# A two-layer hybrid trunk on one core: the second mixer's front in another order of ScalarE and VectorE, and the first mixer's recurrence with fewer VectorE operations

## The reference, cut to what matters

```python
for layer in range(2):
    h = h + (even_mixer if layer == 0 else odd_mixer)(rmsnorm(h, mix_norm[layer]))
    h = h + squared_relu_mlp(rmsnorm(h, mlp_norm[layer]))
return rmsnorm(h, final_norm)

# even_mixer: p = h @ w_in; attention; conv + silu on q, k; then in chunks of 128 tokens
C_loc = einsum('bnlh,bnlhk,bnlhv->bnhkv', wgt, kc, vc)              # n_loc alike, without v
C, m = exp(gl + m - m_new) * C + exp(ml - m_new) * C_loc, m_new     # state before each chunk
w_intra, w_inter = exp(dlog - m_t), exp(b + m_prev - m_t)
qk = (qc @ kc^T) * w_intra
num = qk @ vc + w_inter * (qc @ C_prev)
den = sum(qk) + w_inter * (qc @ n_prev)
hm = num / max(|den|, exp(-m_t))                                    # per head
y_ml = head_layernorm(hm) * ml_norm * sigmoid(o)                    # mean and variance over 128
return concat(y_att, y_ml) @ w_out

# odd_mixer: z, xbc, dt, (r, k, v, wd, ad, gd) = parts of h @ w_in
xbc = silu(causal_conv(xbc)); y = ssd_chunked(xs, dt, A, B, C) + d * xs; y_ssm = norm(y * silu(z))
rw = rw + (token_shift(rw) - rw) * mu
decay = exp(-exp(w_log(tanh(wd) @ w2))); a = sigmoid(a0 + ad @ a2)
kk = kh * k_k / max(sqrt(sum((kh * k_k)**2)), 1e-12); kh = kh * (1 + (a - 1) * k_a)
S = S * w_t - (S @ kk_t) b_t + v_t k_t;  y_t = S @ r_t              # b = kk * a
y_rw = (head_layernorm(y) + bonus) * g
return concat(y_ssm, y_rw) @ w_out
```

## Time and profile before

| | |
|---|---|
| median of 3 runs | 1412.69 us (1411.59 to 1414.43) |
| the profiled execution | 1419.52 us, its span 1417.7 us |
| TensorE busy | 1335.1 us (94% of the span), 6461 matmuls |
| VectorE, ScalarE, GpSimd busy | 582.6, 530.9, 657.2 us |
| granted clock over the span, share of full speed | 0.966 |

### The profile page before, as it was taken

One profiled execution on the slowest core, in us unless ns is written; L12 is line 12 of the kernel. 1 busy time (PEld: TensorE's weight loads), 2 busy tenths in 40 slices (PEclk: granted clock), 3 DMA queues, 4 the chain that ended last, 5 costly groups with the idle time before them and its releaser, 6 DMA issues.

```text
span 1417.7 us, 17835 instructions
## 1 busy us (share of the span) xinstructions
PE 1335.1 (94%) x6461; PEld 1072.1 (76%) x6461; DVE 582.6 (41%) x957; ACT 530.9 (37%) x860; POOL 657.2 (46%) x810
## 2 busy tenths in 40 slices
PE   5999968999999999999788998888999999999998
PEld 4777656788888888887467877788878888888886
DVE  4537676421211212345588576364442121121233
ACT  5335643332322413436553534533343132232332
POOL 5653213664554555564335431321355555554552
PEclk9999978999999999999898998999899999999999
DMA  9322101333333333332212310000133333323321
GB/s 273 90 75 60 60 1 43 91 90 99 94 90 90 102 89 89 98 95 75 60 44 61 90 48 28 1 1 2 45 90 104 90 92 102 89 89 102 91 89 60
DMA packets 198034, 109.12 MB, mean 77 GB/s; under 512 B 4570, under 2 KB 195280, under 8 KB 197840
## 3 DMA queue, kind: packets, MB, share of 16 engines
q1 hardware_dynamic: 197552, 108.16, 26.2%
q0 software_dynamic: 416, 0.07, 0.0%
HBM read 106.11 MB, written 2.10 MB: 76 GB/s over the span
## 4 chain that ended last, share of the span: by engine, by line
PE 71%; DVE 9%; ACT 3%; issue 2%; POOL 0%; DVEq 0%; ACTq 0%; POOLq 0%
PE ps L862 20%; PE ps L863 20%; PE ps L864 20%; PE ps L849 1%; PE ps L903 1%; PE ps L904 1%; PE ps L905 1%; DVE late L2471 1%; DVE arena L2255 1%; PE ps L1278 1%; PE ps L1289 1%; PE ps L1267 1%; PE ps L1146 1%; PE ps L1264 1%; PE ps L1332 0%
## 5 line engine op out<-in xcount | busy, mean ns | idle before, releaser
L771 POOL TENSOR_TENSOR w_lo<-raw_w,w_hi 128x256 fp32r<-128x256 f32 x760 | 613.4, 839 | 620.4 <-ACT w_hi L1386 620.4
L1386 ACT ACTIVATE w_hi<-raw_w 128x1024 fp32r<-128x1024 f32 x190 | 201.1, 1058 | 553.2 <-PE ps L864 441.1
L862 PE MATMUL ps<-hn_hi,w_hi 128*128 128x512 f32 x880 | 359.2, 408 | 11.2 <-POOL w_lo L771 9.5
L863 PE MATMUL ps<-hn_lo,w_hi 128*128 128x512 f32 x880 | 351.7, 400 | 0.0
L864 PE MATMUL ps<-hn_hi,w_lo 128*128 128x512 f32 x880 | 351.3, 399 | 0.0
L862 PE MATMUL ps<-hid_hi,w_hi 128*128 128x512 f32 x576 | 228.4, 397 | 0.0
L863 PE MATMUL ps<-hid_lo,w_hi 128*128 128x512 f32 x576 | 228.3, 396 | 0.0
L864 PE MATMUL ps<-hid_hi,w_lo 128*128 128x512 f32 x576 | 228.3, 396 | 0.0
L862 PEld LDWEIGHTS ps<-hn_hi,w_hi 128*128 128x128 f32 x880 | 167.6, 190 | 61.5 <-issue 18.8
L863 PEld LDWEIGHTS ps<-hn_lo,w_hi 128*128 128x128 f32 x880 | 167.5, 190 | 41.8 <-issue 2.9
L864 PEld LDWEIGHTS ps<-hn_hi,w_lo 128*128 128x128 f32 x880 | 167.5, 190 | 40.9
(11 more groups left out here) (371 smaller groups left out, 1365.5 us busy)
## 6 DMA issues: line engine op xcount, KB each, us to landing
raw_w<-in_w_up SPq DMA_DIRECT2D x64, 512.0 KB, 4.0
raw_w<-in_w_down SPq DMA_DIRECT2D x64, 512.0 KB, 3.7
raw_w<-in_o_w_in SPq DMA_DIRECT2D x27, 512.0 KB, 3.7
raw_w<-in_e_w_in SPq DMA_DIRECT2D x19, 512.0 KB, 3.8
raw_w<-in_e_w_out SPq DMA_DIRECT2D x8, 512.0 KB, 3.7
raw_w<-in_o_w_out SPq DMA_DIRECT2D x8, 512.0 KB, 3.5
rwkv_raw<-in_x SPq DMA_DIRECT2D x4, 512.0 KB, 8.1
out<-arena SPq DMA_DIRECT2D x8, 256.0 KB, 2.9
```

What stands on the lines that cost most here:

```text
L771: nc.gpsimd.tensor_tensor(w_lo[:, n % CUT, ks], raw_w[:, n % RING, ks], w_hi[:, n % CUT, ks].bitcast(F32), ALU.subtract).then_inc(w_cut, 1)
L862: mm(o, a_hi, b_hi, start=(k == 0), stop=False)
L863: mm(o, a_hi, b_lo, start=False, stop=False)
L1386: A(w_hi[:, n % CUT], raw_w[:, n % RING], ACT.Copy).then_inc(w_high, 1)
```

## The change

**First mixer.** `inter` is added in PSUM onto `num`. For that q carries its weight beforehand: ScalarE takes the exponential straight from `m_row` (`q_exp`, four operations for each of chunks 1, 2, 3) and GpSimd multiplies it with q. The denominators and the moments are read in PSUM, and the division is taken into the gain that ScalarE applies when it writes the normalised chunk (`ml_normed`, four operations). `c_loc` takes one bank, its state one to three operations. `k_tok` is turned inside the attention's steps and `k_w` is made from PSUM by two operations. ScalarE's copies of the attention half stand ahead of the sigmoid, VectorE's `low_first` behind `ml_weights(0)`. Lower half tile 0 of the out projection stands behind chunk 1, and half tiles 1, 2 and 3 behind chunk 3, all ahead of the turns of `y_ml`.

**Second mixer.** The LoRA products, gates and decays come a slot or so earlier, the sum for kk's norm one slot earlier; VectorE takes slots 9 and 10 among the receptance parts, the first four channels' silu is one slot later on ScalarE, the last steps of the substitution and its two transposes stand ahead of `take_staged(17)`, and the multiplication by z's silu stands behind the first chunk's solve instead of ahead of it. The other banks move with the round-robin.

```diff
+        if u == 9:
+            for a in range(2):
+                yield "k_tok", a
+        if u == 7:
+            yield "q_exp", 1
...
-    behind = {0: [("norm", 2), ("norm_tok",)], 1: [("turn", ("dt",))], 3: [("lora", 0)],
-              4: [("lora", 1), ("lora", 2), ("a_cum",)], 5: [("lora", 3)], 7: [("kk_sum",)],
+    behind = {0: [("norm", 2), ("norm_tok",)], 1: [("turn", ("dt",))], 3: [("lora", 0), ("lora", 1)],
+              4: [("lora", 2), ("lora", 3), ("a_cum",)], 6: [("kk_sum",)],
...
+    out_banks = [[0, 7, 5, 6, 1, 2, 3, 4], list(range(8))]
+    turned_banks = [[1, 2, 3, 4], [4, 5, 6, 7]]
...
+                for par in range(2):
+                    put("num", n, par, bank=1 + 2 * (n % 2) + par)
+                if n == 1:
+                    put_out(0, 0)
+            for j in range(1, 4):
+                put_out(0, j)
+            put_turned(0, "y_ml")
...
+                        for t in range(1, NT):
+                            pool.wait_ge(S["wi_made"], t)
+                            nc.gpsimd.tensor_tensor(q_w[:, t - 1], q_w[:, t - 1], conv_out[:, 0:2, t * P:(t + 1) * P],
+                                                    ALU.mult).then_inc(S["q_weighted"], 1)
...
-                            ins = mm(o[:, par * 129:(par + 1) * 129], qkw[:, n % 2, hh * P:(hh + 1) * P],
-                                     v_ml[:, n, hh, :], start=True, stop=True)
+                            ins = mm(o[par][:, a * 129:(a + 1) * 129], qkw[:, n % 2, hh * P:(hh + 1) * P],
+                                     v_ml[:, n, hh, :], start=(a == 0), stop=(n == 0), skip_group_check=True)
...
+                        pe.wait_ge(S["q_weighted"], n)
...
-                                ins = mm(o[par][:, a * 129:(a + 1) * 129], conv_out[r, a, tok], c_state[r, n, a, :],
-                                         start=True, stop=True)
+                                ins = mm(o[par][:, a * 129:(a + 1) * 129], q_w[r, n - 1, a, :], c_state[r, n - 1, a, :],
+                                         start=False, stop=True, skip_group_check=True)
...
-                for j in range(3):
+                                    close(ins, "num", n, par)
+                    if n == 1:
+                        half_tile(0, 0, 0)
+                for j in range(1, 4):
                     half_tile(0, j, 0)
                 pe.wait_ge(S["y_ml_gated"], NT - 1)
                 pe.wait_ge(S["y_ml_ready"], 1)
                 for f in range(4):
                     turn(("y_ml", f), [o_gate[:, n, f * P:(f + 1) * P] for n in range(NT)])
-                half_tile(0, 3, 0)
...
+                elif kind == "q_exp":
+
+                    act.wait_ge(S["wl_ready"], u + 1)
+                    o = full(act, "m_row", u).rearrange("p (a b t) -> p a b t", a=2, b=2)
+                    for a in range(2):
+                        for par in range(2):
+                            r = slice(64 * par, 64 * par + 64)
+                            hh = 2 * a + par
+                            ins = A(q_w[r, u - 1, a, :], o[r, a, par, :], ACT.Exp, scale=-1.0,
+                                    bias=marr[r, u, hh:hh + 1])
+                    ins.then_inc(free_sem("m_row", u), 1)
+                    drained(act, "m_row", u)
+                    act.sem_inc(S["wi_made"], 1)
...
+            for u in range(8):
+                drained(act, "att", u)
+            for k in range(4):
+                A(hid_hi[:, k, :], y_mix[:, k, :], ACT.Copy).then_inc(high, 1)
...
+            def ml_normed(n):
+
+                act.wait_ge(S["ml_normed"], n + 1)
+                for par in range(2):
+                    o = full(act, "num", n, par)
+                    for a in range(2):
+                        j = 4 * n + 2 * par + a
+                        ins = A(w_ml[:, n, 2 * a + par, :], o[:, a * 129:a * 129 + P], ACT.Identity, scale=mv[:, j, 1:2],
+                                bias=mv[:, j, 0:1])
+                    ins.then_inc(free_sem("num", n, par), 1)
...
+                ml_root(n)
+                ml_normed(n)
...
                 if j == 3:
                     act.wait_ge(S["omka_ready"], 1)
                     gates_of(0)
+                    gates_of(1)
                 if j == 4:
-                    gates_of(1)
                     gates_of(2)
+                    gates_of(3)
                 if j == 5:
-                    gates_of(3)
                     decay_exps(0)
+                    decay_exps(1)
                 if j == 6:
-                    decay_exps(1)
                     decay_exps(2)
-                if j == 7:
                     decay_exps(3)
                     A(e_s, e_a, ACT.Exp, scale=-DECAY_K).then_inc(S["scales"], 1)
...
-                    drained(act, "bonus")
                     A(a_turned[0:64, :], o[0:64, 0:P], ACT.Copy).then_inc(free_sem("a_turn"), 1)
-                if j == 14:
+                if j == 15:
...
+                        link(V.tensor_tensor(c_tmp, c_state[:, n - 1], over(keep_gain[:, n, :], 2, 129), ALU.mult))
+                    o = full(dve, "c_loc", n)[:, 0:258].rearrange("p (a v) -> p a v", a=2)
+                    if n:
+                        for a in range(2):
+                            ins = V.scalar_tensor_tensor(out=c_state[:, n, a, :], in0=o[:, a, :],
+                                                         scalar=new_gain[:, n, a:a + 1], in1=c_tmp[:, a, :],
                                                          op0=ALU.mult, op1=ALU.add)
...
+            def ml_moments(n):
...
+                o = [full(dve, "num", n, par)[:, 0:258].rearrange("p (a v) -> p a v", a=2) for par in range(2)]
+                for par in range(2):
+                    ins = V.tensor_scalar(d2[:, par, :].unsqueeze(2), o[par][:, :, P:P + 1], -1.0, None, ALU.mult)
...
+                link(V.tensor_tensor(d2, d2, em_arg[:, n, :].rearrange("p (a b) -> p b a", b=2), ALU.max))
+                V.reciprocal(d, d)
+                for par in range(2):
+                    for a in range(2):
+                        ins = V.bn_stats(st6[:, 2 * par + a, :], o[par][:, a, 0:P])
+                link(ins)
+                for j in range(4):
+                    ins = V.bn_aggr(mv[:, 4 * n + j, :], st6[:, j, :])
+                link(ins)
+                var = mv[:, 4 * n:4 * n + 4, 1]
+                link(V.tensor_tensor(var, var, d, ALU.mult))
+                V.tensor_tensor(var, var, d, ALU.mult).then_inc(S["hm_done"], 1)
+
+            def ml_gains(n):
+
+                mean, gain = mv[:, 4 * n:4 * n + 4, 0], mv[:, 4 * n:4 * n + 4, 1]
+                dve.wait_ge(S["ln_root"], n + 1)
+                link(V.reciprocal(gain, gain))
+                link(V.tensor_tensor(gain, gain, dn[:, n % 2, :], ALU.mult))
+                V.scalar_tensor_tensor(out=mean, in0=mean, scalar=-1.0, in1=gain, op0=ALU.mult, op1=ALU.mult
+                                       ).then_inc(S["ml_normed"], 1)
             ml_weights(0)
+            for k in range(4):
+                low_first(0, k, y_mix[:, k, :])
             for n in range(NT):
                 if n + 1 < NT:
                     ml_weights(n + 1)
-                if n == 2:
-                    for k in range(4):
-                        low_first(0, k, y_mix[:, k, :])
-                ml_combine(n)
                 if n:
-                    ml_out(n - 1)
-            ml_out(NT - 1)
+                    ml_gains(n - 1)
+                ml_moments(n)
+            ml_gains(NT - 1)
+            drained(dve, "num", NT - 1, 0)
+            drained(dve, "num", NT - 1, 1)
+            dve.wait_ge(S["o_gained"], NT)
+            V.tensor_tensor(o_gate[:, NT - 1, :], o_gate[:, NT - 1, :], w_ml[:, NT - 1].rearrange("p h t -> p (h t)"),
+                            ALU.mult).then_inc(S["y_ml_ready"], 1)
...
             running_decay(0)
+            running_decay(1)
             take_staged(3)
             shift(3)
-            running_decay(1)
...
             key_part(3)
+            take_staged(9)
             receptance_part(0)
+            conv_staged(9)
             receptance_part(1)
-            take_staged(9)
+            take_staged(10)
             receptance_part(2)
-            receptance_part(3)
-            conv_staged(9)
...
-            take_staged(10)
+            receptance_part(3)
...
-            substitute(23, 24)
+            substitute(23, 31)
+            V.transpose(inv_rows, sub_inv.rearrange("p t c -> p c t"))
+            link(V.transpose(inv_cols, sub_inv))
+            dve.sem_inc(S["inv_ready"], 1)
...
-            substitute(28, 31)
-            V.transpose(inv_rows, sub_inv.rearrange("p t c -> p c t"))
-            link(V.transpose(inv_cols, sub_inv))
-            dve.sem_inc(S["inv_ready"], 1)
...
-            for n in range(NT):
-                drained(dve, "z_tok", n)
-                V.tensor_tensor(xs_tok[:, n, :], xs_tok[:, n, :], z_tok[:, n, :], ALU.mult).then_inc(S["z_silu"], 1)
-            dve.wait_ge(S["z_silu"], NT)
...
```

(5 more changed lines are left out.)

214 lines of the change are left out of this document (74 added, 140 removed).

## The result

The changed kernel has a median of 1399.28 us over 4 runs (1397.91 to 1401.18), beside 1413.56 for the kernel before: 14.3 us less, a ratio of 0.9895 (95% interval 0.9871 to 0.9920). The forecast was 1386, with 1375 to 1401 as its range. The sign and the places were right; the size was 26.6 us where 14.3 came, outside the forecast's own range of 1380 to 1393 and inside the wider one that takes the rivals in.

The account below looks back on a forecast made before the run. TensorE's matmuls, one behind the other, held 71% of the chain, so only other engines' places in it could be shortened. Gains 7.6 + 9.4 + 9.6 = 26.6 off 1412.7 gave 1386 us, range 1380 to 1393, with rivals 1375 to 1401.

Parts of the forecast that it names:

- A: First mixer: ScalarE and two numerators' ring cause TensorE waits of 5 us or more at num(2), num(3); 1392, chance 0.13.
- B: Second mixer's front: bound by VectorE's work, not its waits; only kk's part and the end gain; 1395, chance 0.14.
- D: Slower: in the tighter front, VectorE's 128x512 operations beside GpSimd cost 0.45 us more each; 1418 at 70, chance 0.04.
- First mixer, 7.6 predicted: First mixer: VectorE no longer last, upper half tiles start at 226.0 instead of 233.6; gain 7.6 us, bounds 2 and 12.
- the walk: First mixer: step-by-step timing of the new chain through ScalarE, VectorE and TensorE, from attention's tail to upper half tiles at 226.0.
- the rule on PSUM operands: First mixer's bn_stats: PSUM reads put at 0.07 us more each; at a doubling, 0.22 each, the gain would be 5.8.
- Second mixer up to slot 14, 9.4 predicted: Second mixer's front: fewer waits bring b_tok's turn from 794.25 to 784.8 us; gain 9.4, bounds 3 and 14.
- (a): Second mixer's front: kk_sum, last decays and root one slot earlier bring kk_inv to 696.2 from 698.69; 2.5 us.
- (b): Second mixer, from kk_inv: VectorE's waits for block copies and conv scaling go; 6.7 less 0.5 of new waits, 6.2 us.
- (c): Second mixer's front: a further 0.7 us of waits that follow also goes, bringing b_tok's turn to 784.8.
- The cover for the substitution: Second mixer: some 7 us of moved steps and transposes cost nothing, as VectorE idles 16.84 us before 818.93.
- Behind slot 26, 9.6 predicted: Second mixer's end: 5.85 us of waits, 2.9 of clock and about 0.9 in the first solve go; 9.6, bounds 6 and 11.

Follow-up runs that it names:

- first_reorder: Changed kernel with low_first behind ml_weights(1) and half tile 0 behind chunk 2's first products (qk_st, c_loc): 1394.35 us, ratio 0.9858 to the kernel before.
- kk_ahead: Changed kernel with VectorE's reciprocal of kk's norm ahead of shift(6) instead of behind it: 1395.90 us, ratio 0.9865 to the kernel before.
- silu_mid: Changed kernel with the first four channels' silu right behind ScalarE's cut at slot 15, ahead of the scaling: 1402.90 us, ratio 0.9919 to the kernel before.
- sub_less: Changed kernel with ten of the 31 substitution steps (10 to 19) left out, so part of the computation is missing: 1391.59 us in one run.
- no_end: Changed kernel with substitution steps and transposes spread as before and z's product ahead of the first solve again: 1410.98 us, ratio 0.9955 to the kernel before.
- no_front: Changed kernel with the second mixer's order of before from slot 3 to 15, its end as changed: 1404.04 us, ratio 0.9912 to the kernel before.
- sub_spread: Changed kernel with only the substitution's last steps and transposes spread over slots 17 to 21 again: 1404.21 us, ratio 0.9910 to the kernel before.
- z_ahead: Changed kernel with only z's product ahead of the first solve again: 1409.89 us, ratio 0.9955 to the kernel before.
- best2: Changed kernel with low_first behind ml_weights(1), half tile 0 behind chunk 2's first products, and kk's reciprocal ahead of shift(6): 1394.16 us, ratio 0.9850.
- pool_light: Changed kernel with GpSimd's first-mixer product of the gate with ml_norm cut to 8 of 512 columns: 1398.73 us in one run.

## Why the prediction came out as it did

The median of 1399.28 is 13 us above the forecast, and above the figures of rivals A (1392) and B (1395) too. A did not come: the waits at num(2) and num(3) were 3.87 and 3.24, under its 5. B came in part: behind kk_inv VectorE had hardly a wait for ScalarE left, and its work set the pace. D's sign did not come: VectorE's mean for 128x512 from kk_inv to b_tok's turn went from 0.82 to 0.83 us, not to 1.1. Term by term:

**First mixer, 7.6 predicted, 5.3 in the trace, 3.8 timed.** The mechanism was right: VectorE left the chain, the ring of two numerators made the new waits (3.87 and 3.24 where 3 each were said), the turns of y_ml came without a wait at full clock. Mis-sized were two steps of the walk. The attention's tail was put at 2 us later; TensorE finished it at 186.2 instead of 182.7, so 3.4. Part of this is the price of q_exp: four of its exponentials took 1.47 us and not the 1.2 that w_exp's price gave, 0.8 us more for the three.

```profile
173.57 1.47 ACT L1613 ACTIVATE rwkv_raw<-ps,small 64x128 f32<-64x128 f32 x4
```

And weights(1) stood behind the hid_hi copies and low_first until 193.7, which I had at 192. VectorE after, around it:

```profile
190.51 2.50 DVE L1899 TENSOR_TENSOR hid_lo<-y_mix,hid_hi 128x512 fp32r<-128x512 f32 x4 [2.03 <-ACT hid_hi L1626]
192.93 0.75 DVE L2167 SCALAR_TENSOR_TENSOR rwkv_raw<-ps,late 128x256 f32<-128x256 f32 x2
...
196.75 0.86 DVE L2203 BATCH_NORM_STATS2 small<-ps 128x6 f32<-128x128 f32 x4
...
198.06 1.05 DVE L2209 TENSOR_TENSOR small<-small 128x4 f32<-128x4 f32 x1
199.14 1.21 DVE L2210 TENSOR_TENSOR small<-small 128x4 f32<-128x4 f32 x1
200.85 0.75 DVE L2167 SCALAR_TENSOR_TENSOR rwkv_raw<-ps,late 128x256 f32<-128x256 f32 x2 [0.51 <-PE ps L1078]
```

inter(1) ended at 196.5, 3.5 late; the half tile behind it found the full clock from its fourth matmul and took 3.6 instead of 5, which gave 1.5 back. first_reorder turned both orders together, and 3.3 us came back; what each is worth alone, no run shows. The tiny products at 198 and 199 are slower than the 0.15 I gave them, but weights(2) then waited 0.51 for TensorE, so they cost nothing here. One reading was off: chunk 1's L2153 took 1.89 us in the kernel before, not the 1.18 of chunk 2, so the change took 0.7 more from VectorE than I counted.

The question put to the rule on PSUM operands is settled by L2203: four bn_stats from PSUM took 0.86, from SBUF 0.87. There was no price for these. The Trainium skill ("VectorE: DVE Perf Modes", "Rules for kernel authors") offers a copy to SBUF where many operations follow as the other choice beside the slower rate from PSUM; for these four reads the copy would have bought nothing.

**Second mixer up to slot 14, 9.4 predicted, 5.5 in the trace (10.8 less 5.3).** (a) kk's part was 1.3, not 2.5. The step that failed is "the sum still has to pass ScalarE [...] and the reciprocal": the walk let the reciprocal follow ScalarE's root at once, but it stood behind shift(6) in VectorE's queue, which waited 5.57 us for a scaling that ScalarE did only after the root and the next cut. VectorE after:

```profile
687.12 0.75 DVE L2264 SCALAR_TENSOR_TENSOR rwkv_raw<-relu,cols,rwkv_raw 128x512 f32<-128x512 f32 x1 [5.57 <-ACT rwkv_raw L1662]
...
688.77 3.34 DVE L2352 RECIPROCAL arena<-arena 8x512 f32<-8x512 f32 x1
```

The root had been done since 685.5, 9.3 us earlier than before. kk_ahead took 2.8 back. (b) From kk_inv to b_tok's turn 95.6 us became 91.3: 4.3, not 6.9. The waits that I named did go; VectorE's idle time over this stretch fell by 5.7, where I had 6.2. But its busy time rose by 1.5, from 78.04 to 79.49:

```profile
692.17:783.47 91.30, 84.83 (x385) 64.68 (x386) 79.49 (x116) 37.66 (x66) 40.13 (x41) 0.90 0.22 61
```

That is in part rival D's mechanism at a small scale: of its 68 operations of 128x512 19 took over 0.95 us, where there had been 17, and their sum rose by 0.8; the rest is in smaller ones. (c) The 0.7 of waits that follow did not come, since TensorE got waits of 2.75 and 1.62 for the silu instead. In (b) I had put the condition that the silu only moves its wait by a slot; it did move, from VectorE to TensorE, though silu_mid and sub_less show that removing it alone gives nothing while VectorE's work stands behind it.

**The cover for the substitution held.** Its last steps and transposes ended at 800.6 us in the trace after, with VectorE idle behind them.

**Behind slot 26, 9.6 predicted.** From the end of slot 26 (a lead of 7.6) to the gate product (16.5) the trace has 9.0; no_end has 8.9 and timed 8.5. d started at 861.81 from a slot end at 847.9, 13.9 us, against 21.2 before. One step was off: the turns take 2.42 at the full clock, not the 1.8 that I got from halving 3.67. From d to the gate product 9.5 us became 7.7, twice the 0.9 that I gave to the higher clock there, which made up for it.

**Between slot 14 and slot 26** the prediction had no term, and 3.2 us of the lead went: 10.8 at b_tok's turn, 7.6 at the end of slot 26. These slots have the same matmuls in both kernels; in the 40 us behind b_tok's turn the granted clock was 0.91 in the changed kernel and 1.00 before. That the new wait of 1.62 at 783.47 brought it down is not shown: no_front has no such wait and needs the same 64.4 us.

**The base.** The sum was laid on the profiled execution and 6.8 taken off for the median. The 22.0 between the two spans would be close to the 26.6, but 5.5 of them arose behind the gate product, where nothing is changed, as the last section shows. They could be most of the 6.8 by which that execution of before lay above its median, but no trace of a faster execution of before is there to show it.

## What to carry to other kernels

When a chain is taken off one engine, walk the new chain through every in-order queue it touches, and ask of each instruction ahead of the one that matters what that one waits for: both mis-sized steps were an operation behind something it did not need (the reciprocal behind shift(6), weights(1) behind low_first), and each gave about 3 us in the trace when the order was turned. Where VectorE was busy 94% of a stretch, moving ScalarE's silu out of TensorE's way gave nothing (silu_mid), while less work for VectorE (sub_less) or an earlier start of its chain (kk_ahead) did. And compare two traces by the start of the same work, not by their spans, and better still by the length of one stretch in several traces: the same code differed by 2 us at the second norm and by 3.2 between slots 14 and 26.

## What the runs showed of the hardware

**The clock differs in a stretch where all kernels do the same.** From the gate product to the turns of y_rw TensorE has the same matmuls in every kernel. In the 14 traces of this study it took 114.4 to 114.6 us (seven kernels, the changed one among them), 117.4 to 117.7 (five), or 120.0 and 120.1 (before and kk_ahead): three levels, some 3 us apart. Windows of the granted clock show where, each over the same 76 matmuls ahead of the turns of y_rw. Before, then after, then kk_ahead:

```profile
987.00:1006.00 19.00, 18.74 (x76) 16.72 (x77) 5.21 (x9) 2.16 (x4) 1.35 (x2) 0.67 0.00 1
```

```profile
971.00:984.00 13.00, 12.92 (x76) 11.30 (x77) 5.20 (x9) 1.99 (x4) 1.35 (x2) 1.00 0.00 0
```

```profile
965.50:984.60 19.10, 18.58 (x76) 16.58 (x77) 5.21 (x9) 2.43 (x4) 1.37 (x2) 0.67 0.00 0
```

So 13 us became 19. kk_ahead and after have the same code there, so this is no effect of an edit in that place. All three have the same wait of 0.75 at its start, and then TensorE's first matmuls at the lower level (0.79 us for two) or at the higher (0.49). TensorE before, then after:

```profile
987.26 0.79 PE L1325 MATMUL ps<-arena,rwkv_raw 128*128 128x128 f32 x2 [0.75 <-ACT arena L1380]
```

```profile
971.08 0.49 PE L1344 MATMUL ps<-arena,rwkv_raw 128*128 128x128 f32 x2 [0.75 <-ACT arena L1399]
```

What decides it stays open. Seven of the nine kernels with the changed end of the second mixer had the quickest level and none of the five in which at least one edit of the end is undone, yet the times don't bear out a fixed price: sub_spread is 8.4 us behind the changed kernel at the turns of y_rw and timed 2.1 behind. Between b_tok's turn and the end of slot 26, too, z_ahead, sub_spread and best2 needed 67.6 us where the changed kernel needed 64.4. Such steps are large enough to spread the runs of one kernel over 8 us (before: 1411.6 to 1419.8 in 17 runs) and to hide an edit worth 3.

**A VectorE operation of 4 elements can take 1 us.** Products of two 128x4 operands in SBUF took 0.16 us alone and 0.95 to 1.21 while GpSimd was at work; pool_light turned one of 1.05 into one of 0.16. The bn_stats at 196.75, which read PSUM, kept their time beside the same GpSimd work, and so did the reciprocal at 196.65, with one operand in SBUF (0.18 us as ever). The Trainium skill ("SBUF — State Buffer", "Who interferes with whom") says that a VectorE instruction with two SBUF inputs contends with a GpSimd instruction that reads SBUF, and calls the shared port pair an exclusive lock. The trace agrees: the product that starts at 205.56 ends at 206.52, just behind GpSimd's, which runs from 205.24 to 206.50.
